# Wider moving tiles for the value pairs, and two result banks instead of three for the HGRN levels, in a four-layer float32 kernel

## What is computed

```python
# layer 0: top-k attention of 8 heads of 64, beside a gMLP gate
q, k, v, iq, ik, iw, u, vg = split_cols(h @ ab_w_in[e], AB_SPLITS)
y_b = gmlp_spatial_gate(gelu(u), gelu(vg), ...)
y = concatenate([dsa_attention(...), y_b]) @ ab_w_out[e]

# layer 1: HGRN2, 8 heads of 128, chunks of 64 tokens, a running state S per head
q, f, i, gate = split_cols(h @ c_w_in[o_i], C_SPLITS)
g = lb + (1 - lb) * sigmoid(f); k = 1 - g
# within a chunk: a[t, s] = sum_d q[t, d] * exp(b[t, d] - b[s, d]) * k[s, d], b = cumsum(log g)
o = rms_norm(hgrn2(q, f, i, lb)) * silu(gate)
y = o @ c_w_out[o_i]

# layers 2 (FoX: forget-gate attention) and 3 (MoBA: ALiBi attention): 12 heads of 64,
# and 4 heads that attend to a memory of 256 rows
mkv = rms_norm(mem) @ w_mem_kv[i]
proj = xn @ w_in[j]                   # q, k, v of 768 columns each, qm of 256
h = h + concatenate([self_out, mem_out]) @ w_out[i]
```

## Time and profile before

| what | us |
|---|---|
| median of 3 runs | 1288.62 (1288.33 to 1289.68) |
| the profiled execution's own time | 1288.97 |
| span of its trace | 1287.2 |
| TensorE busy | 1268.8 |
| VectorE busy | 991.6 |
| ScalarE busy | 740.4 |
| all waits of TensorE's output products on a drain of ab_v | 2.0, once |

### The profile page before, as it was taken

The page is one execution under the profiler, slowest core; times in us unless marked ns, Lnnn a source line. Parts: engine busy times, 40 slices in busy tenths (PEclk is TensorE's granted clock), DMA queues, the critical chain, the costliest instruction groups (busy, mean ns, idle before and its releaser), DMA issues.

```text
span 1287.2 us, 21405 instructions
## 1 busy us (share of the span) xinstructions
PE 1268.8 (99%) x8100; PEld 1125.3 (87%) x8100; DVE 991.6 (77%) x1471; ACT 740.4 (58%) x1089; POOL 17.8 (1%) x34
## 2 busy tenths in 40 slices
PE   8999999999999999999999999999999999999997
PEld 7997888888999988888889888888889997888887
DVE  5898798889788778999997766776776665866665
ACT  5465665555877657655566656544445554644443
POOL 2000000000000001000000000000000000000000
PEclk9999999999999999999999999999999999999999
DMA  9653655556534346665546433655554434556551
GB/s 316 205 161 130 193 197 184 183 193 196 154 110 136 127 149 231 206 207 184 186 130 197 131 132 130 212 184 192 196 196 156 162 141 131 183 193 196 195 185 44
DMA packets 168919, 223.19 MB, mean 173 GB/s; under 512 B 5241, under 2 KB 150785, under 8 KB 168721
## 3 DMA queue, kind: packets, MB, share of 16 engines
q1 hardware_dynamic: 166480, 216.04, 51.3%
q0 software_dynamic: 1936, 5.54, 1.3%
q10 hardware_dynamic: 432, 0.64, 0.1%
HBM read 221.15 MB, written 1.06 MB: 173 GB/s over the span
## 4 chain that ended last, share of the span: by engine, by line
PE 89%; DVE 5%; ACT 2%; DMA 2%; issue 1%; DVEq 0%; SPq 0%; ACTq 0%
PE bank L553 22%; PE bank L385 16%; PE bank L386 15%; PE bank L387 15%; PE bank L556 11%; PE bank L878 2%; DVE wlow L1571 1%; PE bank L647 1%; PE bank L683 1%; ACT whigh L1110 1%; PE bank L669 1%; PE bank L462 1%; DMA raw<-in_ab_w_in 1%; DMA raw<-in_ffn_w_down 1%; PE bank L748 0%
## 5 line engine op out<-in xcount | busy, mean ns | idle before, releaser
L1571 DVE TENSOR_TENSOR wlow<-raw,whigh 128x2048 fp32r<-128x2048 f32 (+1 forms) x203 | 462.5, 2281 | 137.4 <-ACT whigh L1110 137.2
L1110 ACT ACTIVATE whigh<-raw 128x2048 fp32r<-128x2048 f32 x202 | 386.3, 1912 | 237.2 <-PE bank L387 152.7
L553 PE MATMUL bank<-xn,whigh 128*128 128x512 f32 x1312 | 328.1, 392 | 0.0
L553 PEld LDWEIGHTS bank<-xn,whigh 128*128 128x128 f32 x1312 | 238.2, 189 | 44.2
L556 PEld LDWEIGHTS bank<-xn,wlow 128*128 128x128 f32 x1312 | 179.0, 190 | 12.8
L556 PE MATMUL bank<-xn,wlow 128*128 128x256 f32 x1312 | 182.9, 282 | 0.0
L385 PE MATMUL bank<-xn,whigh 128*128 128x256 f32 (+1 forms) x560 | 161.8, 289 | 0.6 <-DVE wlow L1571 0.5
L386 PE MATMUL bank<-xn,whigh 128*128 128x256 f32 (+1 forms) x560 | 158.3, 283 | 0.0
L387 PE MATMUL bank<-xn,wlow 128*128 128x256 f32 (+1 forms) x560 | 158.2, 283 | 0.0
L385 PE MATMUL bank<-whigh,g_high 128*128 128x512 f32 (+1 forms) x356 | 138.7, 390 | 1.3 <-DVE g_low L1725 1.1
L386 PE MATMUL bank<-wlow,g_high 128*128 128x512 f32 (+1 forms) x356 | 138.1, 388 | 0.0
(11 more groups left out here) (293 smaller groups left out, 1739.1 us busy)
## 6 DMA issues: line engine op xcount, KB each, us to landing
raw<-in_ffn_w_up SPq DMA_DIRECT2D x44, 1024.0 KB, 5.1
raw<-in_w_gate_up SPq DMA_DIRECT2D x44, 1024.0 KB, 5.1
raw<-in_ffn_w_down SPq DMA_DIRECT2D x22, 1024.0 KB, 4.9
raw<-in_w_down SPq DMA_DIRECT2D x22, 1024.0 KB, 4.9
raw<-in_c_w_in SPq DMA_DIRECT2D x16, 1024.0 KB, 5.4
raw<-in_ab_w_in SPq DMA_DIRECT2D x14, 1024.0 KB, 7.7
raw<-in_w_in_fox SPq DMA_DIRECT2D x10, 1024.0 KB, 5.4
raw<-in_w_in_moba SPq DMA_DIRECT2D x10, 1024.0 KB, 5.1
```

The lines of the kernel that those rows point to most:

```text
L553: pe.matmul(o[:, :].rearrange("p (h t) -> p h t", h=2), wh[:, k, j * P:(j + 1) * P], xn[:, :, k, :], start=k == 0, stop=False)
L1110: act.activation(whigh[s][:, 0:w], raw[s][:, 0:w], ACT.Copy).then_inc(w_high, 1)
L1571: dve.tensor_tensor(wlow[s][:, 0:w], raw[s][:, 0:w], whigh[s][:, 0:w].bitcast(F), ALU.subtract).then_inc(w_low, 1)
```

## The change

1. Twelve units (vg0, vg1 of layer 0; i0 to i3, g2, g3 of layer 1; v0, v1 of layers 2 and 3) are loaded as half of the rows by 512 columns and multiplied by the new `unit_half`, 24 matmuls of 512 columns each. A pair of them fills two banks, one for each token tile, over both units. ScalarE's new `pair_taken` empties the two with one instruction each; a new semaphore `half_used` sets the first unit's buffers free.
2. In layer 1 the ring has four banks (0, 1, 2, 3), the levels only 4 and 5.
3. `OUT_BANKS` has another order for layers 0 and 1.
4. The mix layers' units come as q0 k0 v0 v1 q1 k1 q2 k2 v2, and `BEGIN` follows.
5. `mem` and `memT` are loaded once `gate_ready` has reached 12 (the first group of the second FFN is gated), behind the loads of `f_bias`. ScalarE squares tile 0 after the second group and tile 1 after the last, right ahead of the root.

```diff
     OUT_TILES = {0: (4, 6, 0, 2), 1: (0, 2, 4, 6), 2: (6, 0, 2, 4), 3: (6, 0, 2, 4)}
-    OUT_BANKS = {0: (0, 1, 6, 7), 1: (0, 1, 2, 3), 2: (0, 1, 6, 7), 3: (0, 1, 7, 6)}
+    OUT_BANKS = {0: (1, 6, 7, 0), 1: (0, 3, 1, 2), 2: (0, 1, 6, 7), 3: (0, 1, 7, 6)}
...
     def level_bank(i):
 
-        return 3 + i % 3 if i < 33 else 4 + (i + 1) % 2
+        return 4 + (i + 1) % 2
...
-    BEGIN = (0, 1, 2, 3, 5, 6, 8, 9)
+    BEGIN = (0, 1, 2, 3, 6, 7, 8, 9)
+    MIX_UNITS = [(name, int(n)) for name, n in "q0 k0 v0 v1 q1 k1 q2 k2 v2".split()]
...
+        def unit_half(u, name, banks, half, between=None):
+
+            fetched(u)
+            s = u % RING
+            wh = whigh[s][:, :].rearrange("p (k c) -> p k c", k=KT // 2)
+            wl = wlow[s][:, :].rearrange("p (k c) -> p k c", k=KT // 2)
+            for t in range(TT):
+                if t and between is not None:
+                    between()
+                if half == 0:
+                    fill(name + (t,), banks[t])
+                f = FILLS[name + (t,)]
+                for kk in range(KT // 2):
+                    k = KT // 2 * half + kk
+                    last = split3(psum[f.bank][:, :], xn_high[:, k, t * P:(t + 1) * P], xn_low[:, k, t * P:(t + 1) * P],
+                                  wh[:, kk, :], wl[:, kk, :], half == 0 and kk == 0, half == 1 and kk == KT // 2 - 1)
+                if half:
+                    last.then_inc(bank_full[f.bank], 1)
+            if half:
+                USED[u] = (bank_full[f.bank], f.now, 0)
+            else:
+                last.then_inc(half_used, 1)
+                halves[0] += 1
+                USED[u] = (half_used, halves[0], 0)
...
-        ring_banks[0] = (0, 1, 2)
+        ring_banks[0] = (0, 1, 2, 3)
...
-        pool.dma_start(mem[:, :, :], A["mem_2"][0].rearrange("(t p) d -> p t d", p=P)).then_inc(mem_loaded, 16)
-        pool.dma_start(memT[:, :, :], A["memT"]).then_inc(mem_loaded, 16)
...
+        pool.wait_ge(gate_ready, GROUPS + 1)
+        pool.dma_start(memT[:, :, :], A["memT"]).then_inc(mem_loaded, 16)
+        pool.dma_start(mem[:, :, :], A["mem_2"][0].rearrange("(t p) d -> p t d", p=P)).then_inc(mem_loaded, 16)
...
+        def pair_taken(name, dst, func=ACT.Copy):
+
+            for t in range(TT):
+                o, empty = full(name + (t,))
+                act.activation(dst[:, t, :], o[:, :], func, scale=rstd[:, t:t + 1]).then_inc(empty, 1)
...
-            for t in range(TT):
-                group(t)
-                if l == 1:
-                    if t == 0:
-                        act.wait_ge(mem_loaded, 32)
-                    link(act.activation(xs[:, t, :], mem[:, t, :], ACT.Square, accum_out=sumsq[:, t:t + 1]))
+            group(0)
+            group(1)
+            if l == 1:
+                act.wait_ge(mem_loaded, 32)
+                act.activation(xs[:, 0, :], mem[:, 0, :], ACT.Square, accum_out=sumsq[:, 0:1])
...
             group(GROUPS - 1)
             if l == 1:
+                link(act.activation(xs[:, 1, :], mem[:, 1, :], ACT.Square, accum_out=sumsq[:, 1:2]))
                 act.activation(rms[:, :], sumsq[:, :], ACT.Sqrt, bias=eps[:, 0:1], scale=1.0 / D).then_inc(mem_rms, 1)
...
+                if (name, j) in HGRN_PAIRED and j % 2:
+                    pair_taken((name, 1, "pair", j // 2), (h_i if name == "i" else h_gate)[:, :, 512 * (j // 2):512 * (j // 2 + 1)])
```

More of the change, by code:

```diff
@@ L264, in tall, with half_rows @@
         return w.rearrange("(k p) c -> p k c", p=P)[:, :, c0:c0 + n]
+    def half_rows(w, c0, half):
+        return [(tall(w, c0, 512)[:, KT // 2 * half:KT // 2 * (half + 1), :], 256)]
     def columns(w, lo, hi):
@@ L332, in build @@
             segment(("f", l), columns(w, 3 * SELF, qm))
-        for j in range(3):
-            for n, name in enumerate(("q", "k", "v")):
-                segment((name, l, j), columns(w, n * SELF + 256 * j, n * SELF + 256 * (j + 1)))
+        for name, j in MIX_UNITS:
+            at_ = "qkv".index(name) * SELF + 256 * j
+            segment((name, l, j), half_rows(w, 2 * SELF, j) if name == "v" and j < 2 else columns(w, at_, at_ + 256))
         rows = A["w_out_2"][l - 2].rearrange("(f p) c -> p f c", p=P)
@@ L391, in _ @@
         ring = [0]
+        halves, pair_banks = [0], [None]
         def high_first(o, wh, wl):
@@ L819, in _ @@
                 name, j = AB_UNITS[u]
-                unit = unit_tokens if name in ("v", "vg") else unit_columns
-                unit(FIRST[name, 0, j], (name, 0, j), bank4(), xn_high, xn_low, between=values)
+                if name == "vg":
+                    if j == 0:
+                        pair_banks[0] = (bank4(), bank4())
+                    unit_half(FIRST[name, 0, j], (name, 0), pair_banks[0], j, between=values)
+                else:
+                    unit = unit_tokens if name == "v" else unit_columns
+                    unit(FIRST[name, 0, j], (name, 0, j), bank4(), xn_high, xn_low, between=values)
             if u == 1:
@@ L929, in _ @@
                 name, j = HGRN_UNITS[u]
-                unit = unit_columns if name in "fq" else unit_tokens
-                unit(FIRST[name, 1, j], (name, 1, j), bank4() if u else 6, xn_high, xn_low, between=between)
+                if (name, j) in HGRN_PAIRED:
+                    if j % 2 == 0:
+                        pair_banks[0] = (bank4(), bank4())
+                    unit_half(FIRST[name, 1, j], (name, 1, "pair", j // 2), pair_banks[0], j % 2, between=between)
+                else:
+                    unit = unit_columns if name in "fq" else unit_tokens
+                    unit(FIRST[name, 1, j], (name, 1, j), bank4() if u else 6, xn_high, xn_low, between=between)
             if u == 0:
@@ L964, in values @@
                         if s == BEGIN[j] + 2:
-                            emptied(("mv", l) if kind == "memory" else ("v", l, p // 2))
+                            if kind == "memory":
+                                emptied(("mv", l))
+                            elif p < 4:
+                                for t in range(TT):
+                                    emptied(("v", l, t))
+                            else:
+                                emptied(("v", l, 2))
                             pair_values(l, j, f_mv if kind == "memory" else f_v)
@@ L969, in _ @@
                     out_unit(l, s - 9, 6 + 3 * (l - 2), accs, values)
+                elif name == "v" and n < 2:
+                    if n == 0:
+                        pair_banks[0] = (bank4(), bank4())
+                    unit_half(FIRST["v", l, n], ("v", l), pair_banks[0], n, between=values)
                 elif name == "v":
@@ L1391, in silu @@
             def silu(tile, names, done):
-                for name, j in names:
-                    emptied((name, 1, j))
+                for name in names:
+                    emptied(name)
                 act.activation(tile, tile, ACT.Silu).then_inc(done, 1)
@@ L1433, in _ @@
                 act.activation(h_k[:, pair, :], h_g[:, pair, :], ACT.Identity, bias=1.0, scale=-1.0).then_inc(key_ready, 1)
-            if u < 16 and name in "ig":
+            if u < 16 and name in "ig" and (name, j) not in HGRN_PAIRED:
                 dst = h_i if name == "i" else h_gate
@@ L1498, in _ @@
                         high(FIRST["out", l] + s - 9 + RING)
+                elif name == "v" and n < 2:
+                    if n:
+                        pair_taken(("v", l), f_v[:, :, 0:512])
+                    high(FIRST["v", l, n] + RING)
                 elif name == "v":
```

30 lines of the change are left out of this document (15 added, 15 removed).

## The result

| | before | after |
|---|---|---|
| median of 6 runs, us | 1289.10 (1288.33 to 1289.84) | 1293.74 (1292.79 to 1296.84) |
| ratio | | 1.004, 95% interval 1.003 to 1.005 |
| profiled execution, us | 1288.97 | 1293.66 |
| span of its trace, us | 1287.2 | 1291.8 |

A forecast was written before the change was run, and what follows sets the result against it. TensorE, busy 1268.8 of 1287.2 us, was taken as the bound. The terms -3.2 + 7.3 - 2.05 + 0.15 = +2.2 us gave 1290.8 us, in a wide range of 1283.2 to 1295.2 and a narrow one of 1289 to 1292.5.

The forecast's parts named there:

- the sign of its sum: Whole kernel: slower by 2.2 us; slower had the largest chance, 0.41, against same 0.39 and faster 0.20.
- the six places: HGRN: TensorE waits for late level copies before levels 9, 11, 17, 20, 27 and 31, +7.3 us together.
- the spare bank: HGRN, faster rival: the third level bank was not needed, few or no waits; 1286.3 or 1283.5 us; chance 0.23.
- every wait in full: HGRN, slower rival: the six waits cost 9.3 us and its half units' 1.6 is lost; 1294.4 us; chance 0.15.
- the narrow range: Whole kernel: 1289 to 1292.5 us, with level waits of 6 to 8.5 us; chance 0.50.
- Part 2, two level banks: HGRN: each level waits for the copy of level i-2 instead of i-3, +7.3 us, bounds 0 and 9.3.
- Part 1, the halves: Twelve weight units: 24 matmuls of 512 columns replace 48 of 256, saving 0.27 us each, 3.2 us in all.
- Part 3: Layer 0's first output product: bank 0 is asked for fourth, so a 2.03 us stand goes, saving 2.05 us.
- Part 4: Mix layers: the new order of units costed at nothing, worth 0.3 us either way.
- Part 5: FFN 1: later memory loads save 1.1 us, the square before the root costs 1.24; net +0.15 us.
- The rival of late memory rows: FFN 1: loads over 15.6 us make ScalarE stand after group 1; 1293.8 us with 18.6 us; chance 0.05.

The follow-up runs named there:

- the repetition of before: The kernel before, unedited, timed and profiled once more: 1288.91 us.
- best parts' kernel: Changed kernel with three level banks, ring of three, g2, g3 and FoX in 256 columns, both memory squares after the second FFN group: 1283.94 us.
- two level banks only: The kernel before with only the levels moved to banks 4 and 5, the ring still 0, 1, 2: 1297.77 us, ratio 1.007.
- three level banks: The changed kernel with levels back in banks 3, 4, 5, a ring of three, layer 1's output banks 1, 3, 2, 0, half units kept: 1290.65 us.
- copies a step earlier: The changed kernel with VectorE and ScalarE copying level i-2 instead of i-3 at each step, two level banks kept: 1298.25 us.
- squares early: The changed kernel with both squares of the memory rows after the second FFN group, none at the FFN's end: 1292.68 us.

## Why the prediction was right, and where its size was off

The forecast had the sign of its sum, the six places, and a wide range that held the time. That range ran over 12 us, from the spare bank to every wait in full, so that it held is no great merit. The likeliest number was 1290.8, the narrow range ended at 1292.5, and the time is 1293.7; the waits were not paid in full, so it isn't the slower rival that came true either. The change is +4.6 and not +2.2. Of the 2.4 us between, 0.5 are in HGRN, 0.4 in FFN 1, 0.8 in FoX and 0.25 in MoBA, less 0.15 in mixer 0, and 0.6 are left that may be the clock, which the sum does not have. Step by step,

- **Part 2, two level banks: right.** Forecast +7.3; 7.3 as distances in the changed kernel, 7.0 without the halves. The way of reading it worked: each level's start beside the end of the copy that it will need, and then whether the late engine is tied to TensorE. "The third bank was spare" (0.23) was wrong since it argued from the mean of busy time.
- **Part 1, the halves: mis-sized.** Forecast 3.2 for twelve units. Measured 0.6 for the two of mixer 0 (119.18 against 119.79 from the spread of rstd), 0.75 for HGRN's six under late copies, 0.87 for four of them with three level banks (155.34 against 154.47), 0.3 for the two of MoBA: about 1.9 in all with FoX's 0.3 where its load is in time. The forecast took the step inside a long row of matmuls, 0.1195 and 0.2278, for all of them. In mixer 0, where nothing stands between the matmuls of a pair, that is right and gives 0.3 a unit. Where level or head work stands between token tiles, a unit saves less: 0.23 in HGRN (above), 0.19 in MoBA (two tiles 5.85 us against 6.04), as the steps behind such work are longer (0.32, then 0.23 to 0.24). That makes about 2.7 for twelve, an estimate. Most of the rest went into the longer stands before levels, 0.55. The Trainium skill's gap of N/2.4 ns and 2.5 ns (TensorE: Matmul & The Clock Gate, "Back-to-back issue gap") would have made the part 0.7, an estimate, and the trace speaks against it for these matmuls: the 48 of mixer 0's pair are 0.227 us apart on average (60.10 us on). The 216 ns that the Trainium skill has for 512 columns do stand in the trace for the bf16 warming matmuls (0.216 us apart once they go fast); the float32r ones are longer.
- **Part 3: right.** Forecast -2.05, measured -2.05 in the trace. I had left out what the stand can do to the clock.
- **Part 4: costed at nothing, and nothing shown.** FoX ranged from 102.63 to 103.93 in nine profiles with the new order and 102.91 to 103.22 in four with the old; one load's landing moves it more than the order can be shown to.
- **Part 5: the cost nearly right, the gain mis-sized.** The square costs 1.05 (forecast 1.24) where it was put. The gain of 1.1 was read from one execution: TensorE's idle time at the first down product was 1.08 us in that profile and 0.22 to 0.29 in three others of the same loads. The loads' times are what repeats worst in these traces, and the sum was made against one profile of it. Net +0.55 against the repetition of before instead of +0.15; against the very profile that the forecast had it is -0.3.
- **Left out altogether: the clock.** In six profiles of kernels with two level banks and copies at lag 3, the granted clock was 0.50 for some us in HGRN in four, and each time the stretch was longer: 163.24 and 163.04 with one fall and 164.65 with two, against 161.56 with none. One fall costs 1.5 to 1.7 us there. Three profiles with the levels and the units of before have none. But the best parts' kernel, with no late copy, had one too, so that the late copies bring the falls is likely and not proven. I had priced a stand at its length.

Added up on the repeated before, without any fall in HGRN: -2.75 (mixer 0, without the fall at the start) + 6.2 + 0.55 + 0.3 (FoX) - 0.25 = +4.05. The remaining 0.6 to the measured +4.6 may be the falls of the clock, four in six profiles at 1.5 us, less those that before loses behind the stand for ab_v; that split was not measured by itself. The rival of late memory rows did not come: ScalarE's first square began at 524.45 without a wait.

## What to carry to other kernels

Before a buffer is taken from a rotation, lay the start of every user beside the end of the release that it would then need, from one trace; the short ones, added with what is already waited, came within 0.1 us here, where a mean of busy time misled. Price a term that hangs on one load's landing from several executions, and a stand of TensorE at more than its length, since the clock may fall behind it. Price a change of tile width with the step behind an interruption as well as the one inside a long row. If a wider tile needs more banks held for longer, see first who empties them and what stands ahead of that in its program.

## What the hardware showed that was not expected

- The granted clock fell to 0.50 behind stands of TensorE of very different length: 2.9 us (the changed kernel, at 10.8), 2.03 (two level banks only, 116.1), 1.67 (the same kernel, 399.4), 3.17 (three level banks, 442.9), 2.09 and 1.94 (copies a step earlier, 387.4 and 445.4), and 1.10 (squares early, 453.3). It did not fall behind each such stand: before has the one of 2.03 and no fall in two profiles, and the changed kernel that of 1.67 and none in HGRN. So no length can be read from these traces below which a stand is safe. In the best parts' kernel it fell at 360.7 behind two of 0.61 and 0.52, which the other profiles have too, without a fall:

```profile
360.80:364.10 3.30, 3.30 (x17) 3.30 (x17) 3.30 (x4) 3.30 (x7) 0.00 (x0) 0.50 0.22 77
```

- Stretches with no late load repeated closely over thirteen profiles (FFN 3 and the end: 191.14 to 191.38 us), so that single profiles, cut at fixed places, told more than medians whose ratios are known to 1.2 us at best.
